# Causal mask of the short attention rows: added by VectorE in the score bank, where TensorE multiplied it in

## The chip, the cores and the metric

The kernel runs on one NeuronCore of a Trainium2 chip. A core has four compute engines that run their own instruction streams and meet at semaphores: TensorE (PE in the profile; PEld is its weight load), VectorE (DVE), ScalarE (ACT) and GpSimd (POOL). SyncE (SP) issues the DMAs. The metric is the device time of one execution in microseconds (us). The kernel before takes 1268.92 us, the median of three runs (1268.74 to 1269.92).

## The reference

One layer of a hybrid model on 512 tokens of width 1024, in float32: an input projection, a state-space branch, an attention branch with 16 heads in 4 key groups, a gated mix of the two, and an MLP. The attention branch adds three parts: over compressed keys, over selected blocks (there are 8 blocks and up to 16 are taken, so every causal block is), and over a window of 512 (the whole sequence). So the second and the third part are both plain causal attention, each with its own keys and values (ks, vs and kw, vw):

```python
def masked_softmax(s, m):
    p = jax.nn.softmax(jnp.where(m, s, NEG), axis=-1)
    return p * m
...
        s_s = jnp.einsum('bqgrd,bgqkd->bgrqk', qr, k_sel).astype(jnp.float32) * scale
        p_s = masked_softmax(s_s, m_s)
        o_s = jnp.einsum('bgrqk,bgqkd->bqgrd', p_s.astype(v_sel.dtype), v_sel)
...
        s_w = jnp.einsum('bqgrd,bkgd->bgrqk', qr, kwb).astype(jnp.float32) * scale
        p_w = masked_softmax(s_w, m_w)
        o_w = jnp.einsum('bgrqk,bkgd->bqgrd', p_w.astype(vwb.dtype), vwb)
```

Everything else of the layer is left as it is by the change.

## The kernel before, in words

**Tiling of the attention.** The 512 queries are cut into four blocks i = 0 to 3 of 128 rows. Block i sees (i + 1) * 128 keys, its width: 128, 256, 384 or 512. The work is cut into `PAIRS` = 64 pairs n = 0 to 63: pair n has a half rr = n // 32 of the heads, a query block that falls from 3 to 0 every 8 pairs, a key group g and a branch br (ks or kw). A pair holds two heads. Pairs of width 256 or 128 are called narrow: 16 to 31 and 48 to 63, 32 in all. A narrow pair has both heads side by side in one PSUM bank; a wide pair has a bank for each head.

**One pair, engine by engine.**
- `scores(n)` on TensorE: four products (two heads, the high and the low part of the keys) into the bank, then the causal table: for a narrow pair one product of the identity with the table `causal_bf`, 0 where a key is seen and -1e30 where it isn't, added to both diagonal blocks (line 2216). Its end raises `s_ready`. For a wide pair each head has its own (line 2213).
- `row_max(n)` on VectorE: waits for `s_ready`, takes the maximum of each row and negates it (`nmax`; line 1576 narrow, 1579 and 1582 wide).
- `exp(n, r2)` on ScalarE: the exponential with that bias, and its row sum (line 1004, with a short read of the sum behind it), one for each head.
- `over_sum(n)` on VectorE: one over the sum (`rsum`, line 1590).
- On GpSimd, line 854: the rows times `rsum` and the gate, one for each head (`prob`).
- `turn(n)` on TensorE: transposes (line 2248); `copy_turned` on ScalarE or VectorE (lines 1040, 1601, 1604): out of PSUM; `weigh(n)` on TensorE: times the values (2269), for odd n also the compressed part (2277). Then `high_out` on ScalarE (1011) and `low_out` on VectorE (1610) split the result of two pairs into a high and a low part.

**Order.** It is written out by hand in each engine's stream, and each engine keeps it strictly. `ahead` says how far scores run ahead: at an even narrow n the scores of n + 4 and n + 5 are issued (16 and 17 come at n = 13, 18 and 19 at 14). So two pairs make a round. In a round TensorE runs scores of the next two pairs, turns n and n + 1, weighs n - 2 and n - 1. VectorE runs `row_max` of both new pairs, `over_sum` of n + 2 and n + 3, a copy, `low_out`, and in three of four rounds some steps for the compressed part (`cmp_centre`, `cmp_probs`, `cmp_gates`; lines 1542 to 1568). ScalarE runs a copy, the four exponentials of the new pairs, and `high_out`. After pair 31 the wide pairs 32 to 47 follow, then the narrow pairs 48 to 63 in the same way, and then the state-space groups, the mix, w_o and the MLP.

**Steps on VectorE.** Where an instruction of VectorE needs what the one before it wrote, `step(...)` raises a semaphore of its own (`dve_steps`) and `step.wait()` waits for it.

Of the kernel before, what the change touches and what calls it, by code (L numbers as in the profile page):

```python
# [24 lines left out]
ALU = mybir.AluOpType  # L25
# [3 lines left out]
P = 128  # L29
# [43 lines left out]
K_ID, K_TRI, K_STRI, K_PERM, K_CB, K_CM, K_F = 0, 128, 256, 384, 512, 640, 768  # L73
# [62 lines left out]
def build(nc, a, out):  # L136

    ctx = ExitStack()
    with ctx:
        sem_names = {}  # L140

        def sem(name):
            return ctx.enter_context(nc.semaphore(name))
# [5 lines left out]
        def sb(name, shape, dt=F32, offset=None):  # L149
            size = 4 if dt in (F32, F32R, I32) else 2  # L150
            nbytes = (int(np.prod(shape[1:])) * size + 31) // 32 * 32
            where = at[0] if offset is None else offset
            if offset is None:
                at[0] += nbytes
            assert where + nbytes <= 229344, (name, where + nbytes)
            return nc.alloc_sbuf_tensor_at(name, list(shape), dt, offset=where)

        cst = sb("cst", [P, K_N])
# [7 lines left out]
        ident_bf = sb("ident_bf", [P, P], BF16)  # L166
        causal_bf = sb("causal_bf", [P, P], BF16)
# [73 lines left out]
        kk = [[sb(f"ks{part}", [P, KVG, S], F32R) for part in range(2)]]  # L241
# [16 lines left out]
        q_hl = sb("q_hl", [P, 16, S], F32R)  # L258
# [66 lines left out]
        bank = [ctx.enter_context(nc.psum_tensor(f"bank{i}", [P, 512], F32)) for i in range(8)]  # L325
# [67 lines left out]
        s_ready = sem("s_ready")  # L393
# [93 lines left out]
        def h_bank(k):  # L487

            return bank[(1, 0, 3, 4, 5, 6, 7, 2)[k]]
# [7 lines left out]
        def pair(n):  # L497

            return n // 32, NC - 1 - n // 8 % 4, n // 2 % 4, n % 2

        def width(n):
            return (pair(n)[1] + 1) * P

        def narrow(n):
            return width(n) <= 256
# [801 lines left out]
        def _(dve):  # L1307
            step = Steps(dve, dve_steps)
            V = nc.vector
# [38 lines left out]
            turned, less, part = (bank[2][:, i * P:(i + 1) * P] for i in (0, 2, 3))  # L1348
# [60 lines left out]
            for j in range(12):  # L1409
                u = U_KV + j  # L1410
# [11 lines left out]
                elif kind in (2, 4):  # L1422
                    b = kind // 4
# [147 lines left out]
            def row_max(n):  # L1571
                w, at_step = width(n), 2 * n % 16
                b, off = score_place[n][0]
                dve.wait_ge(s_ready, scored[n][0])
                if narrow(n):
                    V.tensor_reduce(nmax[:, at_step:at_step + 2], bank[b][:, 0:2 * w].rearrange("p (r k) -> p r k", r=2),
                                    AX.X, ALU.max, negate=True).then_inc(max_ready, 1)
                else:
                    V.tensor_reduce(nmax[:, at_step:at_step + 1], bank[b][:, 0:w], AX.X, ALU.max,  # L1579
                                    negate=True).then_inc(max_ready, 1)  # L1580
                    dve.wait_ge(s_ready, scored[n][1])
                    V.tensor_reduce(nmax[:, at_step + 1:at_step + 2], bank[score_place[n][1][0]][:, 0:w], AX.X, ALU.max,
                                    negate=True).then_inc(max_ready, 1)
# [29 lines left out]
            for u in range(6):  # L1613
# [7 lines left out]
                if u in (2, 4):  # L1621
                    cmp_read(0, u // 2 - 1)
            assert ahead[0] == [0, 1]
            row_max(0)
            cmp_centre(0)
            low_q(4)
            over_sum(0)
            cos_q(6)
            rope_q(5)
            row_max(1)  # L1630
            cmp_probs(0)
            cmp_gates(0)
# [400 lines left out]
        def _(pe):  # L2033
            T = nc.tensor
# [24 lines left out]
            for c in range(NC):  # L2059
                if c == 2:  # L2060
# [5 lines left out]
                             start=True, stop=True).then_inc(vec_turned, 1)  # L2066
                pe.wait_ge(xn_ready, c + 1)
                for k in range(KT - 1):
                    mm = T.transpose(h_bank(k)[:, c * P:(c + 1) * P], xn[:, c, k * P:(k + 1) * P], ident)
# [3 lines left out]
            for c in range(NC):  # L2073
                mm = T.transpose(h_bank(KT - 1)[:, c * P:(c + 1) * P], xn[:, c, D - P:D], ident)
# [37 lines left out]
            for j in range(12):  # L2112
                u = U_KV + j
# [5 lines left out]
                if j == 2:  # L2119
                    pe.wait_ge(unit_read[1], 1)  # L2120
                    for c in range(NC):
                        mm = T.transpose(bank[4][:, c * 48:(c + 1) * 48], ag[:, c * P:(c + 1) * P],
                                         ident[0:48, 0:48])
# [9 lines left out]
                if j == 10:  # L2133
                    pe.wait_ge(dta_spread, 3)
                    pe.wait_ge(kvc_ready, 2)
                    for c in range(NC):
                        mm = T.matmul(bank[2][:, c * P:(c + 1) * P], dta_wide[:, c, :], tri, start=True, stop=True)
# [3 lines left out]
                if j == 7:  # L2141
                    pe.wait_ge(hid_ready, 1)
                    for half in range(2):
                        mm = T.matmul(bank[2][:, 0:P], w2c[:, 0, half].rearrange("p e d -> p (e d)"),
                                      hid[:, 0, half].rearrange("p g k -> p (g k)"), start=(half == 0), stop=(half == 1))
                    mm.then_inc(kvc_summed, 1)
                if j == 11:

                    pe.wait_ge(hidr_ready, 1)
                    for g in range(KVG):  # L2150
                        for half in range(2):
                            mm = T.matmul(bank[3][:, g * HD:(g + 2) * HD], hidr[:, half, g].rearrange("p e k -> p (e k)"),
                                          w2c[:, 1, half].rearrange("p e d -> p (e d)"),
                                          start=(half == 0), stop=(half == 1))
# [41 lines left out]
            def scores(n):  # L2196
                rr, i, g, br = pair(n)
                pp, e = divmod(g, 2)
                w = width(n)
                for r2 in range(2):  # L2200
                    u = rr * 4 + 2 * pp + r2
                    b, off = score_place[n][r2]
                    if i == NC - 1 and br == 0:
                        pe.wait_ge(qlo_ready, 2 * u + 2)
                    if r2 == 0 or not narrow(n):
                        if score_free[n][r2]:
                            pe.wait_ge(exp_ready, score_free[n][r2])
                    for part in kk[br]:
                        T.matmul(bank[b][:, off:off + w], q_hl[:, 2 * u + e, i * P:(i + 1) * P], part[:, g, 0:w],  # L2209
                                 start=(part is kk[br][0] and off == 0), stop=(part is kk[br][1]),  # L2210
                                 skip_group_check=narrow(n))
                    if not narrow(n):
                        T.matmul(bank[b][:, i * P:(i + 1) * P], ident_bf[:], causal_bf[:],
                                 start=False, stop=True, skip_group_check=True).then_inc(s_ready, 1)
                if narrow(n):
                    T.matmul(bank[b][:, 0:2 * w].rearrange("p (r k) -> p r k", r=2)[:, :, i * P:(i + 1) * P], ident_bf[:],
                             causal_bf[:].unsqueeze(1).to_broadcast([P, 2, P]),
                             start=False, stop=True, skip_group_check=True).then_inc(s_ready, 1)

            def turn_to(k):  # L2220

# [284 lines left out]
            def turn_h2(k, c):  # L2506
                return T.transpose(h2_bank(k)[:, c * P:(c + 1) * P], xn2[:, c, k * P:(k + 1) * P], ident)


            for n, c in enumerate(WO_ORDER):  # L2510
                pe.wait_ge(xn2_first, n + 1)
                for k in range(KT // 2):
                    mm = turn_h2(k, c)
# [3 lines left out]
            for k in range(KT // 2, KT):  # L2517
                for c in range(NC):
                    mm = turn_h2(k, c)
# [72 lines left out]
```

## Time and profile before

| what | value |
|---|---|
| median of three runs | 1268.92 us |
| time of the profiled execution | 1269.1 us |
| its span | 1267.3 us |
| PE busy | 1247.1 us (98%) |
| DVE busy | 762.4 us (60%) |
| ACT busy | 583.3 us (46%) |
| POOL busy | 406.9 us (32%) |
| granted TensorE clock, mean | 0.998 |

The span runs from the first to the last instruction; the device time lies 1.8 us above it. Matmul ends are modelled in the profile, so a PE that reads 98% busy still has short gaps. The two narrow stretches lie at 205 to 241 us and at 282 to 317 us of the span.

### The profile page before, as it was taken

The page shows a single profiled execution, that of the slowest core. Times are in us where ns is not written, and L with a number is a line of the kernel's source. Part 1 is how long each engine was busy: PE and PEld are TensorE (multiplying, and loading weights), DVE is VectorE, ACT ScalarE, POOL GpSimd, SP SyncE. Part 2 cuts the span into 40 slices and gives each one's busy share as a digit, 9 for nine tenths or more (in the row PEclk, how much of TensorE's full clock was granted, in tenths as well). Part 3 has the DMA queues.
Part 4 walks back from the last instruction along what each step waited for, and adds up shares of the span by engine and source line. Part 5 has one row for each costly group of instructions (what it writes and reads, how often), then busy time and mean ns, then how long its engine had stood idle before and what let it go on. Part 6 is the DMA issues. An engine that isn't in the chain of part 4 may idle for free.

```text
span 1267.3 us, 19175 instructions
## 1 busy us (share of the span) xinstructions
PE 1247.1 (98%) x6732; PEld 1026.6 (81%) x6732; DVE 762.4 (60%) x1352; ACT 583.3 (46%) x1016; POOL 406.9 (32%) x271
## 2 busy tenths in 40 slices
PE   9999999999999999999999999999999999999997
PEld 7887877677888888888888888888878888888885
DVE  6845887775577877787874111111048849479487
ACT  6325476666544544454433222222366345254364
POOL 3433354545333333333333444444430110201200
PEclk9999999999999999999999999999999999999999
DMA  8523410000222222232222333334453061340601
GB/s 244 159 70 71 94 38 2 1 2 2 67 69 78 70 83 66 66 83 66 68 81 79 89 99 100 99 99 123 144 182 100 19 215 32 129 136 17 208 7 66
DMA packets 172312, 108.40 MB, mean 86 GB/s; under 512 B 25220, under 2 KB 163814, under 8 KB 172262
## 3 DMA queue, kind: packets, MB, share of 16 engines
q1 hardware_dynamic: 172022, 107.65, 29.2%
q8 instruction: 30, 0.49, 0.2%
q14 instruction: 20, 0.16, 0.0%
q10 hardware_dynamic: 240, 0.09, 0.0%
HBM read 104.84 MB, written 2.10 MB: 84 GB/s over the span
## 4 chain that ended last, share of the span: by engine, by line
PE 87%; DVE 4%; ACT 4%; issue 2%; POOL 1%; DMA 1%; SPq 0%; DVEq 0%; ACTq 0%; POOLq 0%
PE bank L2424 21%; PE bank L2046 17%; PE bank L2433 10%; PE bank L2050 9%; PE bank L2528 8%; PE bank L2533 4%; PE bank L2269 2%; PE bank L2443 2%; PE bank L2209 2%; PE bank L2248 2%; POOL prob L854 1%; PE bank L2106 1%; PE bank L2449 1%; PE bank L2404 1%; ACT prob L1004 1%
## 5 line engine op out<-in xcount | busy, mean ns | idle before, releaser
L834 POOL TENSOR_TENSOR wlo<-raw,whi 128x1024 fp32r<-128x1024 f32 x133 | 324.9, 2443 | 694.0 <-ACT whi L1082 388.5
L1082 ACT ACTIVATE whi<-raw 128x1024 fp32r<-128x1024 f32 x96 | 101.7, 1060 | 295.6 <-PE bank L2433 160.0
L2046 PE MATMUL bank<-h_hi,whi 128*128 128x512 f32 x488 | 194.5, 398 | 0.7 <-DVE h_lo L1323 0.7
L2046 PE MATMUL bank<-h_lo,whi 128*128 128x512 f32 x488 | 190.4, 390 | 0.0
L2424 PE MATMUL bank<-h_hi,whi 128*128 128x512 f32 x384 | 150.3, 391 | 1.3 <-DVE grp L1766 0.7
L2424 PE MATMUL bank<-h_lo,whi 128*128 128x512 f32 x384 | 149.5, 389 | 0.0
L2050 PE MATMUL bank<-h_hi,wlo 128*128 128x512 f32 x488 | 120.8, 390 | 0.0
L2046 PEld LDWEIGHTS bank<-h_hi,whi 128*128 128x128 f32 x488 | 91.8, 188 | 21.2 <-DVE h_lo L1323 2.5
L1854 DVE TENSOR_TENSOR mt<-bank,sig 128x512 f32<-128x512 f32 x16 | 11.1, 691 | 161.6 <-PE bank L2433 161.6
L1746 DVE SCALAR_TENSOR_TENSOR grp<-bank,vt,grp 128x511 f32<-128x511 f32 (+2 forms) x96 | 71.8, 748 | 58.9 <-ACT grp L1106 49.9
L2050 PEld LDWEIGHTS bank<-h_hi,wlo 128*128 128x128 f32 x488 | 91.6, 188 | 19.0
L2046 PEld LDWEIGHTS bank<-h_lo,whi 128*128 128x128 f32 x488 | 91.8, 188 | 17.6
L854 POOL TENSOR_SCALAR prob<-prob,rsum,gate 128x512 f32<-128x512 f32 (+3 forms) x128 | 79.5, 635 | 80.3 <-DVE rsum L1590 80.3
L2433 PE MATMUL bank<-h_hi,wlo 128*128 128x512 f32 x384 | 94.9, 389 | 0.0
L2424 PEld LDWEIGHTS bank<-h_hi,whi 128*128 128x128 f32 x384 | 72.1, 188 | 18.5 <-DVE h_lo L1894 2.7
L2433 PEld LDWEIGHTS bank<-h_hi,wlo 128*128 128x128 f32 x384 | 72.1, 188 | 15.0
L2424 PEld LDWEIGHTS bank<-h_lo,whi 128*128 128x128 f32 x384 | 72.1, 188 | 14.6
L1004 ACT ACTIVATE prob<-bank,nmax 128x512 f32<-128x512 f32 (+3 forms) x128 | 66.8, 535 | 37.1 <-DVE nmax L1579 33.8
L1234 ACT ACTIVATE whi<-raw 128x1024 fp32r<-128x1024 f32 x30 | 31.7, 1057 | 79.2 <-PE bank L2433 60.9
L1917 DVE TENSOR_TENSOR comb<-comb 128x256 f32<-128x256 f32 x64 | 30.2, 493 | 49.5 <-ACT comb L1272 49.0
L1967 DVE TENSOR_TENSOR x<-bank,x 128x512 f32<-128x512 f32 x64 | 41.1, 684 | 21.2 <-PE bank L2533 21.2
L2248 PE MATMUL bank<-cst,prob 128*128 128x128 f32 x320 | 48.6, 278 | 3.1 <-POOL prob L854 1.4
(318 smaller groups left out, 2502.2 us busy)
## 6 DMA issues: line engine op xcount, KB each, us to landing
raw<-in_w_in SPq DMA_DIRECT2D x75, 512.0 KB, 3.8
raw<-in_w_up SPq DMA_DIRECT2D x32, 512.0 KB, 4.1
draw<-in_w_down SPq DMA_DIRECT2D x16, 1024.0 KB, 6.5
raw<-in_w_ssm_branch SPq DMA_DIRECT2D x16, 512.0 KB, 3.6
raw<-in_w_in SPq DMA_DIRECT2D x20, 256.0 KB, 3.7
raw<-in_w_attn_branch SPq DMA_DIRECT2D x8, 512.0 KB, 3.6
raw<-in_w_o SPq DMA_DIRECT2D x8, 512.0 KB, 3.7
x_sb<-in_x SPq DMA_DIRECT2D x4, 512.0 KB, 5.3
```

The source lines that it names most:

```text
L834: nc.gpsimd.tensor_tensor(wlo[slot][:], raw[slot][:], whi[slot][:].bitcast(F32), ALU.subtract).then_inc(wlo_ready, units)
L854: nc.gpsimd.tensor_scalar(rows, rows, rsum[:, at_step % 16:at_step % 16 + 1], gate[:, i, column:column + 1], ALU.mult, ALU.mult).then_inc( ...
L1004: nc.scalar.activation(prob_rows(n, r2), bank[b][:, off:off + width(n)], ACT.Exp, bias=nmax[:, at_step % 16:at_step % 16 + 1], accum_out=e ...
L1082: nc.scalar.activation(whi[slot][:], raw[slot][:], ACT.Copy).then_inc(whi_ready, 1)
L1746: ins = V.scalar_tensor_tensor(grp[:, j, back:S], bank[j % 2][:, 0:S - back], vt[:, bass.ds(tile + (V_CW + (CONV - 1 - back) * 32), 1)], g ...
L2046: T.matmul(bank[slot][:], whi[slot][:, k * P:(k + 1) * P], part[:, k, :], start=(k == 0 and n == 0), stop=False)
L2050: mm = T.matmul(bank[slot][:], wlo[slot][:, k * P:(k + 1) * P], h_hi[:, k, :], start=False, stop=(k == KT - 1))
L2248: mm = T.transpose(to[:, off + t * P:off + (t + 1) * P], prob_rows(n, r2)[:, t * P:(t + 1) * P], ident)
L2424: T.matmul(to[:], whi[slot][:, k * P:(k + 1) * P], part[:, k0 + k, :], start=(start and k == 0 and n == 0), stop=False)
L2433: mm = T.matmul(to[:], wlo[slot][:, k * P:(k + 1) * P], hi[:, k0 + k, :], start=False, stop=(stop and k == KT - 1))
L2528: T.matmul(bank[at_bank + t][:], part[:, 2 * (n % 2) + kl, which, t * P:(t + 1) * P], half_slot(n, 0)[:, kl, :], start=(fresh and n % 2 == ...
L2533: return T.matmul(bank[at_bank + t][:], comb_hi[:, 2 * (n % 2) + kl, which, t * P:(t + 1) * P], half_slot(n, 1)[:, kl, :], start=False, st ...
```

## The change

For a narrow pair TensorE no longer multiplies the table in: its fourth score product raises `s_ready`. VectorE waits for that, adds the float32 table of `cst` (columns `K_CB` on) to the two diagonal blocks of the bank, in place, waits for its own step, and only then takes the maximum. Wide pairs are as before.

```diff
@@ row_max(n), on VectorE @@
                 dve.wait_ge(s_ready, scored[n][0])
                 if narrow(n):
+                    causal = bank[b][:, 0:2 * w].rearrange("p (r k) -> p r k", r=2)[:, :, w - P:w]
+                    step(V.tensor_tensor(causal, causal, cst[:, K_CB:K_CB + P].unsqueeze(1).to_broadcast([P, 2, P]), ALU.add))
+                    step.wait()
                     V.tensor_reduce(nmax[:, at_step:at_step + 2], bank[b][:, 0:2 * w].rearrange("p (r k) -> p r k", r=2),
                                     AX.X, ALU.max, negate=True).then_inc(max_ready, 1)
@@ scores(n), on TensorE @@
                     for part in kk[br]:
-                        T.matmul(bank[b][:, off:off + w], q_hl[:, 2 * u + e, i * P:(i + 1) * P], part[:, g, 0:w],
-                                 start=(part is kk[br][0] and off == 0), stop=(part is kk[br][1]),
-                                 skip_group_check=narrow(n))
+                        mm = T.matmul(bank[b][:, off:off + w], q_hl[:, 2 * u + e, i * P:(i + 1) * P], part[:, g, 0:w],
+                                      start=(part is kk[br][0] and off == 0), stop=(part is kk[br][1]),
+                                      skip_group_check=narrow(n))
...
                 if narrow(n):
-                    T.matmul(bank[b][:, 0:2 * w].rearrange("p (r k) -> p r k", r=2)[:, :, i * P:(i + 1) * P], ident_bf[:],
-                             causal_bf[:].unsqueeze(1).to_broadcast([P, 2, P]),
-                             start=False, stop=True, skip_group_check=True).then_inc(s_ready, 1)
+                    mm.then_inc(s_ready, 1)
```

On TensorE, in round n = 18 (scores of 22, here from its second head on, and of 23, then the transposes of 18), these are the rows before; `causal_bf,ident_bf` is the table product:

```order
L2209 MATMUL bank<-ks_102,q_hl 128x256
L2209 MATMUL bank<-ks_103,q_hl 128x256
L2216 MATMUL bank<-causal_bf,ident_bf 128x2x128
L2209 MATMUL bank<-kw_113,q_hl 128x256
L2209 MATMUL bank<-kw_114,q_hl 128x256
L2209 MATMUL bank<-kw_113,q_hl 128x256
L2209 MATMUL bank<-kw_114,q_hl 128x256
L2216 MATMUL bank<-causal_bf,ident_bf 128x2x128
L2248 MATMUL bank<-cst,prob_112 128x128 x4
```

and these the rows now (line 2212 was 2209, and 2249 was 2248):

```order
L2212 MATMUL bank<-ks_102,q_hl 128x256
L2212 MATMUL bank<-ks_103,q_hl 128x256
L2212 MATMUL bank<-kw_113,q_hl 128x256
L2212 MATMUL bank<-kw_114,q_hl 128x256
L2212 MATMUL bank<-kw_113,q_hl 128x256
L2212 MATMUL bank<-kw_114,q_hl 128x256
L2249 MATMUL bank<-cst,prob_112 128x128 x4
```

Two products less in the round; nothing else stands elsewhere on TensorE. On VectorE, from the `cmp_centre` steps ahead of round n = 18 to the `low_out` of its end, before:

```order
L1542 TENSOR_REDUCE cst_111<-cs 128x8
L1544 TENSOR_TENSOR cs<-cs,cst_111 128x2x128
L1576 TENSOR_REDUCE nmax<-bank 128x2 x2
L1590 RECIPROCAL rsum<-esum 128x2 x2
L1601 COPY pT_128<-bank 128x2x256
L1610 TENSOR_TENSOR o_lo<-bank,o_hi 128x128
```

and now (1577 is the add, 1579 was 1576, 1593 was 1590, 1604 was 1601, 1613 was 1610):

```order
L1542 TENSOR_REDUCE cst_111<-cs 128x8
L1544 TENSOR_TENSOR cs<-cs,cst_111 128x2x128
L1577 TENSOR_TENSOR bank<-bank,cst 128x2x128
L1579 TENSOR_REDUCE nmax<-bank 128x2
L1577 TENSOR_TENSOR bank<-bank,cst 128x2x128
L1579 TENSOR_REDUCE nmax<-bank 128x2
L1593 RECIPROCAL rsum<-esum 128x2 x2
L1604 COPY pT_128<-bank 128x2x256
L1613 TENSOR_TENSOR o_lo<-bank,o_hi 128x128
```

The two maxima that stood side by side now each have an add ahead of them, and the `rsum` of the earlier pairs, the copy and `low_out` stand behind all four.

## Rows read from the trace of the kernel before

**Rows 1.** Windows: engines' busy us (instructions), granted clock, DMA share, GB/s.
```profile
core 0: us, PE busy (x) PEld busy (x) DVE busy (x) ACT busy (x) POOL busy (x), PEclk, DMA share, GB/s
...
205.00:241.00 36.00, 34.62 (x321) 27.31 (x320) 24.92 (x75) 23.88 (x98) 19.33 (x37) 1.00 0.01 1
...
282.00:317.00 35.00, 33.86 (x321) 27.09 (x320) 21.37 (x66) 22.67 (x95) 19.27 (x38) 1.00 0.01 2
```

**Rows 2.** Waits, 205 to 241 us: waiter, awaited, total us, times, longest.
```profile
POOL prob L854 <- DVE rsum L1590: 14.8, 9, 2.7
DVE o_lo L1610 <- ACT o_hi L1011: 6.9, 8, 1.4
...
PEld bank L2248 <- POOL prob L854: 3.3, 9, 0.6
...
ACT prob L1004 <- DVE nmax L1576: 1.7, 3, 1.0
```

**Rows 3.** Chain that ended last, first narrow stretch: start us, us, what.
```profile
220.84 1.11 ACT prob L1004 x5
...
222.46 0.29 DVE o_lo L1610
...
223.65 0.62 DVE nmax L1576 x2
224.44 2.47 POOL prob L854 x4
```

**Rows 4.** Timeline of PE, round 18: start us, us, engine, line, what.
```profile
217.00 0.72 PE L2209 MATMUL bank<-ks,q_hl 128*128 128x256 f32 x4
...
217.60 0.72 PE L2209 MATMUL bank<-kw,q_hl 128*128 128x256 f32 x4
218.16 0.28 PE L2216 MATMUL bank<-causal_bf,ident_bf 128*128 128x256 bf16 x1
218.28 0.49 PE L2248 MATMUL bank<-cst,prob 128*128 128x128 f32 x3
```

**Rows 5.** Single lines: duration ns min/median/max, first and last start us, forms.
```profile
L1714 DVE TENSOR_TENSOR bank<-bank,eo x16: 566/566/567, 367.9 to 668.8; 128x384 f32<-128x384 f32 x16
...
L1371 DVE TENSOR_TENSOR bank<-bank,dtw x1: 299/299/299, 35.4 to 35.4; 128x128 f32<-128x128 f32 x1
```

**Rows 6.** Timeline of DVE: a step, and the instruction that waits for it.
```profile
367.94 0.57 DVE L1714 TENSOR_TENSOR bank<-bank,eo 128x384 f32<-128x384 f32 x1
368.54 0.69 DVE L1717 SCALAR_TENSOR_TENSOR yt<-bank,grp 128x512 f32<-128x512 f32 x1
```

**Rows 7.** Timeline of DVE, round 18.
```profile
218.30 0.29 DVE L1610 TENSOR_TENSOR o_lo<-bank,o_hi 128x128 fp32r<-128x128 f32 x1 [0.67 <-ACT o_hi L1011]
...
219.30 1.28 DVE L1576 TENSOR_REDUCE nmax<-bank 128x2 f32<-128x512 f32 x2
220.50 0.22 DVE L1590 RECIPROCAL rsum<-esum 128x2 f32<-128x2 f32 x2
```

**Rows 8.** Timeline of ACT: first exponentials and the high part behind them.
```profile
220.02 0.47 ACT L1004 ACTIVATE prob<-bank,nmax 128x256 f32<-128x256 f32 x1 [0.50 <-DVE nmax L1576]
...
223.97 0.37 ACT L1004 ACTIVATE prob<-bank,nmax 128x128 f32<-128x128 f32 x1 [1.00 <-DVE nmax L1576]
...
225.36 0.29 ACT L1011 ACTIVATE o_hi<-bank 128x128 fp32r<-128x128 f32 x1
```

**Rows 9.** Timeline of DVE: rsum and maxima in other rounds.
```profile
207.42 0.15 DVE L1590 RECIPROCAL rsum<-esum 128x2 f32<-128x2 f32 x1
...
223.56 0.70 DVE L1576 TENSOR_REDUCE nmax<-bank 128x2 f32<-128x256 f32 x2
...
234.05 0.22 DVE L1590 RECIPROCAL rsum<-esum 128x2 f32<-128x2 f32 x2
```

**Rows 10.** Timeline of POOL, last two groups of rows of the second stretch.
```profile
310.71 1.74 POOL L854 TENSOR_SCALAR prob<-prob,rsum,gate 128x128 f32<-128x128 f32 x4 [1.39 <-DVE rsum L1590]
312.78 1.75 POOL L854 TENSOR_SCALAR prob<-prob,rsum,gate 128x128 f32<-128x128 f32 x4 [0.32 <-DVE rsum L1590]
```

## The prediction

> **What bounds the kernel now.** The windows come first [rows 1]: the change touches two stretches, 36 and 35 us long. TensorE is 34.6 and 33.9 us busy in them, VectorE only 24.9 and 21.4, at the full 2.4 GHz clock (1.00). By shares the change takes work from the bound and gives it to an engine with 11.1 us of room (36.0 - 24.9). The waits contradict the shares [rows 2]: in the first stretch GpSimd waits 14.8 us for `rsum` of VectorE, VectorE 6.9 us for `o_hi` of ScalarE, and TensorE's weight loads 3.3 us for GpSimd. The chain shows what closes [rows 3]: exponentials at 220.84 (behind the maximum of 219.30 [rows 7]), `o_lo` at 222.46, the next maxima at 223.65, then `rsum` and GpSimd at 224.44, and TensorE behind it. That is a loop of VectorE and ScalarE through the hand-written orders: `low_out` waits for `high_out`, which stands behind the four exponentials on ScalarE; these wait for `row_max`, which stands behind the last `low_out`. So VectorE's 6.9 us is mostly the other half of a loop, not room.
>
> **What is removed.** 32 table products. In round 18 the scores of 22 start at 217.00, those of 23 at 217.60, the transposes at 218.28 [rows 4]. Four score products take 0.56 us (217.60 to the table product at 218.16), so 1.28 us for both pairs becomes 8 x 0.14 = 1.12: 0.16 us in a round. There are 16 rounds: 2.6 us, if TensorE set every one. That is the most that this part can give back. `s_ready` also comes 0.11 us earlier, which counts only where `row_max` waits for it.
>
> **What is added.** 32 adds of 128 x 256 in place in PSUM, each with a wait for its own result. The trace has the same form in two sizes: 566 ns for 384 and 299 ns for 128 elements [rows 5]; halfway is 433 ns. The instruction that waits starts 0.03 us behind the end: 367.94 + 0.57 = 368.51 against 368.54 [rows 6]. So a maximum starts 0.47 us later for its own add. Bounds for this: 0.30 (the 128-element form, no gap) and 0.60 (the 384-element form with its gap). I take 0.47, since both sizes stand on one line and 256 lies between them.
>
> Two maxima now run into each other: 1.28 us for both, the `rsum` 1.20 after the first start [rows 7]. An add without a wait would also hide 0.09 us in its neighbour (0.69 long, 0.60 apart). The Trainium skill ("VectorE: DVE Perf Modes", section The DRAIN you can't avoid) says that the next operation does not start before the pipeline is empty, with or without a semaphore. By that rule the wait is free and the add costs 0.43 - 0.09 = 0.34; the row of the step disagrees, since the dependent instruction starts behind the end and the independent maximum before it.
>
> **Which of it lies on the path.** In one round, `rsum` of the earlier pairs stands behind both adds: it is later than the round's start by 2 x 0.47 = 0.94 us. GpSimd and the transposes follow it. The next `low_out` is later by less, as ScalarE overlaps: it starts its first exponential 0.47 later, and then the second pair's maximum can be late too. At width 256 two exponentials take 0.9 us, the second maximum follows the first by 0.60 + 0.47 = 1.07, so 0.17 more; at width 128 the exponentials take 0.7 us (all four 225.36 - 223.97 = 1.39 us [rows 8]); the first maximum ends at 223.97, 0.41 behind its start, and both take 0.70 [rows 9], so the second follows by 0.29 + 0.47 = 0.76, 0.1 more. A round that VectorE leads, which shows as ScalarE idle before its first exponential (three times [rows 2], 0.50 at 220.02 and 1.00 at 223.97 [rows 8]), thus adds 0.6. Where `low_out` waited for something else, that wait takes the delay up first.
>
> Round by round in the first stretch, delay at `low_out` and then at `rsum`:
> - Scores of 16 and 17: the adds follow pair 15's maxima directly. `rsum` at 207.42 [rows 9] comes 0.94 - 0.11 = 0.83 later. The `low_out` behind it waited for ScalarE and takes up about half, so some 0.4 stays.
> - 18 and 19: 0.39, then 1.33. GpSimd is late by that and TensorE's transposes of 15 behind it.
> - 20 and 21: TensorE's scores come 1.33 - 0.16 = 1.17 later; `rsum` 1.17 + 0.94 = 2.11.
> - 22 and 23: `low_out` 1.17 (218.30 [rows 7]), `rsum` at 220.50 later by 2.11. TensorE had waited for GpSimd here already, so it takes the whole.
> - 24 and 25: VectorE leads: 1.17 + 0.64 = 1.81; `rsum` (behind the maxima of 223.56 [rows 9]) 2.75.
> - 26 and 27: it leads again: 1.81 + 0.58 = 2.39; `rsum` 3.3.
> - 28 and 29: `high_out` waits for TensorE, late by 2.75; I take 3.45 for `rsum`, not 3.7, since scores of this round come while VectorE runs its maxima, and part of the wait for them goes.
> - 30 and 31: `low_out` 2.6, `rsum` at 234.05 [rows 9] 3.5.
>
> GpSimd was idle before that last step and TensorE waited for it, so the transposes of 28, the weighing and the scores of 32 are 3.5 us late. The wide pairs behind are bound by TensorE and give nothing back. TensorE's 0.16 a round is in these numbers and mostly lost: it waits for GpSimd instead.
>
> The second stretch has the same order as the first up to the scores of pair 61, and I take the same delays. At its end GpSimd starts its last group 0.32 us after the one before ended [rows 10]. The first of these is 3.4 late (310.71 becomes 314.09); it takes 1.78 and the last then follows without a gap at 315.87 in place of 312.78: 3.1 late, and so are the last transposes and the first product behind the attention.
>
> **Sum.** 3.5 + 3.1 = 6.6 us. The profiled execution, 1269.1 us with a span of 1267.3, would be 1275.7 with a span of 1273.9. The median of the runs lies 0.2 below: 1275.5. With 0.30 for an add instead of 0.47 the sum scales to 4.2 (1273.1), with 0.60 to 8.4 (1277.3); if the joints between rounds take up 1.5 us more or less, that is 1271.6 to 1278.8. Elsewhere in the program nothing moves.
>
> **The rivals.**
> - *TensorE sets the end after all.* VectorE's idle 11.1 us [rows 1] holds 16 x 0.47 = 7.5 us of adds. If that idle time is real room, only the 0.16 us a round is left: 1268.9 - 2.6 = 1266.3, faster. For it speaks TensorE's 34.6 of 36 us; against it GpSimd's 14.8 us of waiting for `rsum` [rows 2] and the loop in the chain. It decides if ScalarE does not wait for the maxima: it did, in the rows quoted.
> - *The joints take up most.* ScalarE waits for the narrow maxima three times only [rows 2]; if the other rounds absorb their 0.94 (the `low_out` waits are up to 1.4 us [rows 2]), 0.6 x 3 a stretch less TensorE's 1.3 is left: 0.5 a stretch, 1270. Against it: `rsum` is delayed in each round directly, and TensorE's loads wait for GpSimd nine times [rows 2].
> - *Nothing is taken up.* Each add delays everything behind it: 32 x 0.47 = 15.0, 1283.9. Against it: ScalarE's four exponentials overlap the second add.
> - *The wait is free*, as by the pipeline rule: 6.6 x 0.34 / 0.47 = 4.8, 1273.7. The row of the step speaks against it.
> - *TensorE's clock falls.* The gaps in which it waits for GpSimd grow from 0.6 [rows 2] to some 1.3 us. The granted clock is 1.00 in both stretches now; no row of this kernel shows the 1.2 GHz level behind such gaps. If a third of one stretch ran at it, its 12 us of products would take up to twice as long: about 1287.
>
> **How the numbers follow.** A measurement of this kernel can tell about 0.2% (2.5 us) from no change: the bounds are 1266.4 and 1271.5. Chances: the forecast 0.66 (own range 1271.6 to 1279); TensorE sets the end 0.06; the joints take up most 0.08; nothing is taken up 0.11; the wait is free 0.05; the clock 0.04. Low end 1270.5, which leaves out the first rival and half of the second; high end 1281, which leaves out the clock and most of the third. Faster 0.06; same 0.08 and 0.01 of the forecast's lower tail; slower 0.85.
>
> **What would show it.** Right: 32 adds of 0.43 us, each maximum 0.03 us behind its add; the second maximum no longer overlapping the first; `rsum` of the eight rounds later by 0.8, 1.3, 2.1, 2.1, 2.75, 3.3, 3.45, 3.5 us against a common start; TensorE's idle time before the transposes larger, released by GpSimd; the first wide scores 3.5 us later, the first product after the attention 6.6 later, and the same lag at the end. Wrong: a narrow stretch no longer than 36.5 us, or one 7 us longer; an add under 0.3 or above 0.6 us; a granted clock under 1.00 in a stretch; a lag that shrinks in the wide pairs or after the attention.

## The result, and the profile after

| | before | after |
|---|---|---|
| median of the runs (6 each) | 1268.93 us | 1276.91 us (1276.06 to 1277.84) |
| ratio to before | | 1.006 [1.0051, 1.007] |
| profiled execution, its span | 1269.1, 1267.3 us | 1276.6, 1274.8 us |
| granted clock, mean of the span | 0.998 | 0.995 |

The changed kernel is slower by 8.0 us, 0.6% and well outside the scatter of either kernel; 6.6 was forecast.

The adds, by their line in the changed kernel (duration ns min/median/max, first and last start us):

```profile
L1577 DVE TENSOR_TENSOR bank<-bank,cst x32: 406/423/433, 205.9 to 317.6; 128x256 f32<-128x256 f32 x32
```

VectorE of the changed kernel at the head of the first stretch and in round 18 (start us, us, engine, line, what), to be laid beside [rows 7, 9]:

```profile
205.89 0.43 DVE L1577 TENSOR_TENSOR bank<-bank,cst 128x256 f32<-128x256 f32 x1
206.36 0.69 DVE L1579 TENSOR_REDUCE nmax<-bank 128x2 f32<-128x512 f32 x1
206.97 0.42 DVE L1577 TENSOR_TENSOR bank<-bank,cst 128x256 f32<-128x256 f32 x1
...
208.03 0.16 DVE L1593 RECIPROCAL rsum<-esum 128x2 f32<-128x2 f32 x1
...
219.00 0.29 DVE L1613 TENSOR_TENSOR o_lo<-bank,o_hi 128x128 fp32r<-128x128 f32 x1 [0.67 <-ACT o_hi L1011]
...
220.00 0.43 DVE L1577 TENSOR_TENSOR bank<-bank,cst 128x256 f32<-128x256 f32 x1
220.46 0.69 DVE L1579 TENSOR_REDUCE nmax<-bank 128x2 f32<-128x512 f32 x1
...
222.13 0.22 DVE L1593 RECIPROCAL rsum<-esum 128x2 f32<-128x2 f32 x2
```

An add is 0.43 us long and its maximum starts 0.03 to 0.04 us behind the end of the add. The two maxima no longer follow each other directly. TensorE in the same round, beside [rows 4]:

```profile
217.70 0.72 PE L2212 MATMUL bank<-ks,q_hl 128*128 128x256 f32 x4
218.26 0.64 PE L2212 MATMUL bank<-kw,q_hl 128*128 128x256 f32 x4
218.74 0.98 PE L2249 MATMUL bank<-cst,prob 128*128 128x128 f32 x6
```

From the scores of 22 to the transposes it now takes 1.04 us (217.70 to 218.74) and took 1.28. The waits, 205 to 244 us (waiter, awaited, total us, times, longest), beside [rows 2]:

```profile
POOL prob L854 <- DVE rsum L1593: 17.4, 9, 2.9
PEld bank L2249 <- POOL prob L854: 8.0, 18, 1.4
...
DVE o_lo L1613 <- ACT o_hi L1011: 5.4, 7, 1.6
ACT prob L1004 <- DVE nmax L1579: 4.2, 5, 1.2
```

TensorE's weight loads waited 3.3 us for GpSimd and now wait 8.0; ScalarE waits 4.2 us for the narrow maxima instead of 1.7. This window is 3 us longer than that of before, as the stretch itself is.

**Where the time went.** Marks in TensorE's timeline of the kernel before: the last wide scores (of the branch kw, the attention over a window) ahead of the first stretch, the transposes of 28, the first wide scores behind the stretch, the last wide scores ahead of the second stretch, and the first product behind the attention.

```profile
204.38 0.59 PE L2209 MATMUL bank<-kw,q_hl 128*128 128x384 f32 x2
...
234.81 1.62 PE L2248 MATMUL bank<-cst,prob 128*128 128x128 f32 x4 [0.35 <-POOL prob L854]
...
237.20 0.71 PE L2209 MATMUL bank<-ks,q_hl 128*128 128x512 f32 x2
...
281.45 0.59 PE L2209 MATMUL bank<-kw,q_hl 128*128 128x384 f32 x2
...
316.67 0.48 PE L2046 MATMUL bank<-h_hi,whi 128*128 128x512 f32 x1
```

The same marks in the changed kernel:

```profile
204.18 0.60 PE L2212 MATMUL bank<-kw,q_hl 128*128 128x384 f32 x2
...
237.74 1.77 PE L2249 MATMUL bank<-cst,prob 128*128 128x128 f32 x4 [1.19 <-POOL prob L854]
...
240.94 1.20 PE L2212 MATMUL bank<-ks,q_hl 128*128 128x512 f32 x2
...
286.43 0.59 PE L2212 MATMUL bank<-kw,q_hl 128*128 128x384 f32 x2
...
324.30 0.47 PE L2049 MATMUL bank<-h_hi,whi 128*128 128x512 f32 x1
```

Against a common first mark (the changed kernel was 0.20 early there) the delay is 237.74 - 234.81 + 0.20 = 3.13 us at the transposes of 28, 286.43 - 281.45 + 0.20 = 5.18 at the second stretch, and 324.30 - 316.67 + 0.20 = 7.83 behind the attention. So the first stretch gives 3.13 and the second 2.65. The 2.05 between them come in the first wide pairs. There two score products of 512 columns take 1.20 us instead of 0.71, and the windows of the changed kernel say why (busy us of the engines PE, PEld, DVE, ACT and POOL, then the granted clock):

```profile
236.00:238.00 2.00, 0.81 (x7) 0.44 (x3) 1.48 (x6) 1.71 (x9) 0.77 (x2) 0.97 0.03 8
238.00:244.00 6.00, 5.95 (x23) 3.66 (x23) 3.56 (x12) 1.94 (x7) 2.72 (x7) 0.50 0.00 0
244.00:246.00 2.00, 2.00 (x16) 1.09 (x14) 1.28 (x3) 1.37 (x4) 0.00 (x0) 0.82 0.00 0
```

The granted clock falls from 1.00 to 0.50 (1.2 GHz) at about 237.9, right behind TensorE's idle 1.19 us before 237.74, and is back at 1.00 some 6.8 us later, at about 244.7.

### The profile page after: what moved, and what is told of

Same layout as the page of the kernel before. It is cut to its first block, busy times and chain, and to the rows that moved or that the text cites. A ratio compares the mean times of both kernels' runs of the same rounds, so it can differ in the third digit from the quotient of the medians.

```text
span 1274.8 us, 19143 instructions
## 1 busy us (share of the span) xinstructions
PE 1249.6 (98%) x6700; PEld 1025.2 (80%) x6700; DVE 775.3 (61%) x1384; ACT 585.6 (46%) x1016; POOL 406.7 (32%) x271
## 4 chain that ended last, share of the span: by engine, by line
PE 87%; DVE 5%; ACT 3%; issue 2%; POOL 1%; DMA 1%; SPq 0%; DVEq 0%; ACTq 0%; POOLq 0%
PE bank L2425 20%; PE bank L2049 17%; PE bank L2434 10%; PE bank L2053 8%; PE bank L2529 8%; PE bank L2534 4%; PE bank L2270 2%; PE bank L2212 2%; PE bank L2444 2%; PE bank L2249 2%; POOL prob L854 1%; PE bank L2109 1%; PE bank L2450 1%; PE bank L2405 1%; PE bank L2316 1%
## 5 line engine op out<-in xcount | busy, mean ns | idle before, releaser
L2249 PE MATMUL bank<-cst,prob 128*128 128x128 f32 x320 | 52.1, 283 | 7.8 <-POOL prob L854 5.6
```

The costliest lines, as they stand in the source:

```text
L2249: mm = T.transpose(to[:, off + t * P:off + (t + 1) * P], prob_rows(n, r2)[:, t * P:(t + 1) * P], ident)
```

## The experiments

Two theories stood at the start. One: the adds stand ahead of `rsum` on VectorE, GpSimd starts later by them, TensorE waits for it, and its own saved products don't count. The other: what costs is TensorE's clock, or an add whose cost doesn't depend on what stands behind it. The letters A, B and C in a forecast below are its own. Each kernel has 5 to 11 runs. The experiments ran in three groups of four, each on another chip, each beside the kernel before: this had 1268.95 us in the first group (the changed kernel again, the gap filled, neither product nor add, the second stretch only), 1269.49 in the second (both, `rsum` ahead, `o_lo` last on the changed kernel) and 1269.29 in the third (the rest). The changed kernel itself ran in the first group alone. Where a later kernel is set against its 1276.62, the two come from different chips, which leaves about 0.5 us open; the ratios are to the kernel before on the same chip.

**The changed kernel again.** No edit.

> The changed kernel once more, beside the three that are compared with it. Expected 1276.9 us again (1276.0 to 1277.9). In its first profile the lag behind the kernel before is 3.1 us at the transposes of pair 28 (237.74 against 234.81, starts of the attention 0.2 apart), 5.2 in the wide pairs and 7.6 at the first product behind the attention; the 2 us between the first two lie where the granted clock was 0.50. Theory A (the clock falls each time behind the gap before the transposes of pair 28): the same 2 us and the same place again. Rival B (a chance event of that one execution): full clock in this profile and a span shorter by 2 us.

Measured: 1276.62 us (1275.94 to 1277.76), 1.006 [1.0046, 1.0074]. Its windows:

```profile
205.00:245.00 40.00, 35.82 (x310) 26.64 (x308) 31.96 (x94) 25.65 (x100) 19.76 (x38) 1.00 0.00 1
...
304.00:310.00 6.00, 5.71 (x37) 4.50 (x38) 4.51 (x14) 3.15 (x14) 3.65 (x7) 0.72 0.01 3
...
318.00:324.00 6.00, 5.37 (x30) 3.62 (x32) 1.67 (x7) 1.75 (x9) 3.28 (x8) 0.72 0.01 3
```

The first stretch kept the full clock; two falls of some 3.4 us each came in the second. So falls recur from execution to execution and their place does not, and neither A nor B of this forecast holds. The marks of this execution price them:

```profile
204.90 0.59 PE L2212 MATMUL bank<-kw,q_hl 128*128 128x384 f32 x2
...
238.45 1.62 PE L2249 MATMUL bank<-cst,prob 128*128 128x128 f32 x4 [1.20 <-POOL prob L854]
...
285.11 0.59 PE L2212 MATMUL bank<-kw,q_hl 128*128 128x384 f32 x2
...
324.68 0.47 PE L2049 MATMUL bank<-h_hi,whi 128*128 128x512 f32 x1
```

Against the common first mark (0.52 late) the delay is 3.12 us at the transposes of 28 and still 3.14 at the second stretch: with the clock at 1.00 the wide pairs add nothing, so the 2.05 us of the first execution go with its fall. Behind the attention it is 7.49, so the second stretch gives 4.35 with two falls where it gave 2.65 with none, 1.7 us for both.

**The gap before the transposes of 28 filled**, with products into the bank that the transposes overwrite.

```
+                if n == 28:
+                    to = turn_to(turn_no[n][0])
+                    for _ in range(5):
+                        T.matmul(to[:], q_hl[:, 0, 0:P], q_hl[:, 0, :], start=True, stop=True)
```

> The changed kernel, with five products of 128x512 on TensorE ahead of the transposes of pair 28, written to the bank that these transposes overwrite and read by nobody; they fill the gap of 1.19 us that TensorE has there (5 x 0.22 us = 1.1). Theory A (the gap lets the clock fall and that costs 2 us): granted clock 1.00 from 236 to 245 us, lag of the wide pairs 3.2 instead of 5.2 us, time 1274.9 us. Rival B (the clock falls by chance or for another reason, or the 2 us are the lag of the loop in another place): 1276.9 us as without the fillers, or 0.1 to 0.3 more.

Measured: 1275.02 us (1274.87 to 1276.31), 1.0049 [1.0035, 1.0063], 1.6 below the changed kernel on the same chip. Both windows of its profile have the full clock:

```profile
205.00:245.00 40.00, 37.02 (x315) 27.46 (x313) 32.13 (x93) 25.70 (x101) 19.75 (x38) 1.00 0.00 1
286.00:325.00 39.00, 35.55 (x308) 27.06 (x307) 28.99 (x86) 23.43 (x93) 18.64 (x36) 1.00 0.01 2
```

The attention ends at 322.47 there, 5.74 us late against the common first mark (204.44): near 3.1 + 2.65, the delay of the two stretches alone. A (1274.9) held. About 1.6 us of the 8.0 go with the filled gap; the marks put them in the clock. The runs of the two kernels overlap at their ends (up to 1276.31 here, from 1275.94 there). That one filled gap takes away falls elsewhere too is not shown: they vary.

**Neither product nor add**: the mask of the narrow pairs is left out.

```
-                    T.matmul(bank[b][:, 0:2 * w]..., ident_bf[:], causal_bf[:]..., start=False, stop=True, ...).then_inc(s_ready, 1)
+                    mm.then_inc(s_ready, 1)
```

> The products of the table are gone and no add takes their place: the causal mask of the 32 narrow pairs is left out of the computation. It shows what TensorE's part of the change is worth alone. Loop theory (VectorE and ScalarE lead the round where ScalarE waits for the maxima, TensorE leads the others): less than the 2.6 us of 16 rounds x 0.16, I expect 1.5 us, 1267.4 us. Rival (TensorE sets the end of every round): 2.6 us, 1266.3 us. Rival (TensorE sets none): 1268.9 us.

Measured: 1267.69 us (1267.47 to 1268.55), 0.999 [0.9981, 0.9999]: -1.26 us. That is all that 32 table products are worth on the path, of 8 x 0.24 + 8 x 0.20 = 3.5 us that they occupy on TensorE (1.28 us less 1.04 in a round of width 256, 1.12 less 0.92 in one of width 128). It lies between the two rivals and near the 1.5 of the forecast.

**Both product and add** (the table is added twice).

```
+                    causal = bank[b][:, 0:2 * w].rearrange("p (r k) -> p r k", r=2)[:, :, w - P:w]
+                    step(V.tensor_tensor(causal, causal, cst[:, K_CB:K_CB + P]..., ALU.add))
+                    step.wait()
```

> The kernel before with VectorE's add and its wait put in, and TensorE's product with the table kept (the table is added twice, so the output is another). It prices VectorE's part alone. Taking TensorE's table product out with no add in its place gave -1.26 us. Theory A (VectorE's add delays rsum, GpSimd starts that much later, and TensorE, waiting for GpSimd anyway, has no time of its own on that path): the product's absence is worth little once the adds are there, so this kernel stands 0 to 1.3 us above the changed one, 1276.6 to 1277.9. Rival B (TensorE's time counts one for one beside the adds): 32 products of about 0.24 us beyond the changed kernel's, 1276.6 + 7.7 = 1284. Rival C (the add alone costs nothing, and what costs is the score bank that is handed over sooner): about 1269.

Measured: 1277.35 us (1276.76 to 1278.14), 1.0063 [1.0049, 1.0077]. With the adds there, TensorE's table products cost 0.7 us against the changed kernel's 1276.62, and 0.2 if each is set against the kernel before on its own chip (7.86 against 7.67): not clear of noise. The forecast priced B twice too high, since 0.24 us is the saving for the two products of a round: at the 3.5 us above, B would stand at 1280.1. It is out at that price too, and so is C: the add on VectorE alone makes the loss.

**Adds in the second stretch only** (pairs 48 to 63; the first keeps its products). VectorE's add has the same condition.

```
-                if narrow(n):
+                if narrow(n) and n >= 48:
```

> The table is added by VectorE for pairs 48 to 63 only; pairs 16 to 31 keep their product on TensorE. The second stretch cost 2.65 us in the changed kernel (lag 4.98 before it, 7.63 behind it). Theory A (each stretch pays for itself, the first one 3.1 in the loop and 2.0 in the clock): 1268.9 + 2.65 = 1271.6 us, clock 1.00 in both. Rival (half of the change costs half, 4 us): 1272.9 us.

Measured: 1272.51 us (1272.29 to 1273.45), 1.0027 [1.0017, 1.0038]: +3.6, between the two forecasts, 0.9 above A and 0.4 below the rival. Its profile has +2.60 from the start of the second stretch to the end of the attention, at full clock, as the changed kernel had 2.65. So the second stretch pays this by itself and doesn't need the first. The profile loses 1.0 us more between 325 and 600 us, where the edit changes nothing and the other profiles lose nothing; where that comes from stays open.

**`rsum` ahead of the adds and maxima**, on the changed kernel and on the kernel before.

```
             for n in range(PAIRS):
+                if ahead[n + 1] and narrow(ahead[n + 1][-1]):
+                    for m in due:          # the pairs whose sums this round owes
+                        over_sum(m)
                 for m in ahead[n + 1]:
                     row_max(m)
```

> The changed kernel with VectorE's reciprocals of the row sums that are due in a round (rsum) put ahead of the round's adds and maxima instead of behind them. In the changed kernel's trace of round 18 the exponentials of these sums had ended at 218.80, rsum started at 222.13, and the adds and maxima that stand ahead of it had started at 220.00: it could start 2.1 us sooner. Theory A (the cost is that rsum, and so GpSimd, stands behind the adds): nearly all of the 7.7 us goes away, and with GpSimd early some of TensorE's waits for it too: 1268, within 1265.5 to 1270.5. Rival B (VectorE's added time itself, or the exponentials behind the later maxima, holds the rounds): each maximum comes 0.14 us later still, about 1277 to 1279. Rival C (both count): halfway, 1272 to 1274.

> The kernel before with the same move of rsum ahead of the round's maxima, and TensorE's table products kept. Theory A: GpSimd's start comes 1.1 to 1.3 us sooner in each round, and TensorE's waits for it in the two stretches (8.1 us of first waits together by the earlier trace) shrink: 1266, within 1263.5 to 1268.4. Rival B (GpSimd's start doesn't hold the rounds of the kernel before, since there TensorE or the exponentials do): the same or up to 1 us more, 1268.9 to 1270.

Measured: the changed kernel 1272.56 us (1272.25 to 1273.89), 1.0028 [1.0017, 1.004], so -4.1 against 1276.62, and 3.1 above the kernel before on its own chip; the kernel before 1266.65 us (1266.28 to 1267.69), 0.9976 [0.9967, 0.9985], so -2.8 (A, 1266, held). VectorE in round 18 of the changed kernel with `rsum` ahead:

```profile
218.21 0.29 DVE L1613 TENSOR_TENSOR o_lo<-bank,o_hi 128x128 fp32r<-128x128 f32 x1 [0.66 <-ACT o_hi L1011]
...
219.20 0.22 DVE L1593 RECIPROCAL rsum<-esum 128x2 f32<-128x2 f32 x2
219.34 0.41 DVE L1577 TENSOR_TENSOR bank<-bank,cst 128x256 f32<-128x256 f32 x1
219.78 0.69 DVE L1579 TENSOR_REDUCE nmax<-bank 128x2 f32<-128x512 f32 x1
```

and one of its waits, 205 to 244 us:

```profile
ACT prob L1004 <- DVE nmax L1579: 6.0, 5, 1.6
```

`rsum` comes 1.0 us behind the start of `o_lo`, not 3.1. But ScalarE's wait for the maxima grew from 4.2 to 6.0 us: that speaks for the other arc of the loop, maxima to exponentials. Theory A said 1268 and fell; the halfway case (C, 1272 to 1274) held. Not all of the gain is the loop's: this profile has the full clock in both stretches, and against the common first mark (204.18) it is 1.67 us late at the second stretch (282.92) and 3.39 behind the attention (319.86). So the stretches cost 1.67 and 1.72 where they cost 3.13 and 2.65: `rsum` ahead takes 2.4 of 5.8 us from the loop, and the 2 us at the lower clock are absent from this execution. The later maxima are the candidate for the 3.4 that stay.

**`o_lo` last in its round**, on the changed kernel and on the kernel before.

```
-                if n % 2 == 1 and n >= 3:
-                    low_out((n - 3) // 2)
                 ...
                 if n % 8 == 5 and n < 61:
                     cmp_gates(n // 8 + 1)
+                if n % 2 == 1 and n >= 3:
+                    low_out((n - 3) // 2)
```

> The changed kernel with VectorE's subtraction o_lo put last in its round, behind the steps of the compressed branch (centre, probs, gates) instead of ahead of them. In the trace of the changed kernel VectorE waits there 0.67 us (219.00) and 0.84 us (223.78) for ScalarE's o_hi, 5.4 us in the first stretch, with 0.8 us of that branch's steps queued behind it that wait for nothing. Theory A (each round's rsum is late by what stands ahead of it on VectorE, waits included): the steps fill the wait, rsum comes 0.4 to 0.8 us sooner in three of four odd rounds, and the time falls by 2 to 4 us, 1272.5 to 1274.6. Rival B (VectorE's wait is slack that comes back elsewhere): the same within 0.5 us, 1276.6.

> The kernel before with o_lo last in its round, rsum where it was. Theory A (rsum's lateness holds this kernel's rounds as well, only less): VectorE's wait for o_hi is filled by the compressed branch's steps, rsum comes 0.4 to 0.7 us sooner, and with rsum ahead of the maxima worth 2.5 us this is worth 1 to 2.5: 1266.5 to 1268. Rival B (in this kernel the maxima and the rsum are early enough): no change, 1269.

Measured: the changed kernel 1272.44 us (1271.59 to 1273.96), 1.0024 [1.0015, 1.0033], so -4.2 against 1276.62, and 3.0 above the kernel before on its own chip; the kernel before 1266.20 us (1265.18 to 1266.92), 0.9975 [0.9966, 0.9984], so -3.1. Both times A's mechanism held and the gain came out just above its range. The move applies to the wide pairs too, so the gain is not the narrow stretches' alone. Round 18 of the changed kernel with this edit:

```profile
218.04 0.41 DVE L1542 TENSOR_REDUCE cst<-cs 128x8 f32<-128x256 f32 x1
218.48 0.45 DVE L1544 TENSOR_TENSOR cs<-cs,cst 128x256 f32<-128x256 f32 x1
218.85 0.28 DVE L1613 TENSOR_TENSOR o_lo<-bank,o_hi 128x128 fp32r<-128x128 f32 x1
219.05 0.42 DVE L1577 TENSOR_TENSOR bank<-bank,cst 128x256 f32<-128x256 f32 x1
```

and its wait:

```profile
DVE o_lo L1613 <- ACT o_hi L1011: 2.0, 2, 1.1
```

The steps of the compressed branch fill the idle 0.67 us ahead of `o_lo`, and the next add starts directly behind it; the wait for `o_hi` goes from 5.4 to 2.0 us. Part of VectorE's idle time was thus a wait with ready work queued behind it.

**Each add twice.**

```
                     step(V.tensor_tensor(causal, causal, cst[:, K_CB:K_CB + P]..., ALU.add))
                     step.wait()
+                    step(V.tensor_tensor(causal, causal, cst[:, K_CB:K_CB + P]..., ALU.add))
+                    step.wait()
```

> The changed kernel with VectorE's add and its wait done twice for each of the 32 pairs (the table is added twice, so the output is another). It asks how much cover VectorE's first add used up. An add and the gap behind it measure 0.46 us (205.89 to 206.36), two in a row 0.43 + 0.46. Theory A (the first add used up what cover there was: GpSimd waits for rsum in every round and starts the moment it comes): the second add passes nearly whole, 32 x 0.45 = 14 us, 1276.6 + 14 = 1291, within 1288 to 1293. Rival B (each add costs what the first did, about half of it covered): 1276.6 + 7.7 = 1284. Rival C (the first's cost was a wait that is paid once a round, whatever its length): under 1280.

Measured: 1294.36 us (1293.17 to 1297.02), 1.0194 [1.018, 1.0208]: +17.7 us over the changed kernel, 0.55 for each of 32 adds that take 0.46 with their gap. The number is above the range of A, and its profile has long falls of the clock, so the sum alone doesn't price a second add. A part at full clock does: from the first exponential of pair 20 to that of pair 24 it takes 231.54 - 220.33 = 11.21 us, and the changed kernel 225.78 - 216.86 = 8.92. Four second adds make 2.29 us, 0.57 each. So no cover is left for a second add, and B and C are out. The windows (the first holds most of that part; how much the falls cost in all is not measured apart):

```profile
218.00:231.00 13.00, 10.81 (x96) 8.20 (x98) 10.59 (x27) 6.68 (x23) 4.35 (x8) 1.00 0.01 2
...
234.00:246.00 12.00, 11.59 (x70) 9.54 (x70) 8.58 (x26) 5.10 (x22) 4.81 (x11) 0.57 0.00 0
```

**Both moves on VectorE**: `rsum` ahead and `o_lo` last.

> The changed kernel with both moves on VectorE: rsum ahead of the adds and maxima, and o_lo last in its round. Each alone gave -4.1 us (1272.56 and 1272.44). Theory A (both shorten the same path, from VectorE's wait for o_hi through rsum to GpSimd; but after the first the exponentials wait for the maxima, 6.0 us of ScalarE's idle time in the first stretch, and that wait the second move takes away): together -6 to -8, 1268.6 to 1270.6, about the kernel before. Rival B (TensorE then has no wait left and its saved table products show): below the kernel before with rsum moved, under 1266.6. Rival C (they remove the same wait): no more than either alone, 1272.

> The kernel before with both moves. With rsum moved alone it took 1266.65, TensorE was busy 39.4 of 40 us of the first stretch and waited for GpSimd 2.0 us in first waits of 0.3 at most. Theory A (TensorE is the bound there): nothing more to be had, 1266.6 within 0.6 us. Rival B (the second stretch, where TensorE was busy 38.2 of 39, and its exponentials' waits for maxima still hold it): 1265.5.

Measured: the changed kernel 1268.81 us (1267.66 to 1271.76), 0.9995 [0.9986, 1.0004]; the kernel before 1264.92 us (1263.87 to 1265.24), 0.996 [0.9947, 0.9974]. On the changed kernel the moves add up for the most part (-4.1, -4.2, together -7.8; against the kernel before on each chip they leave 3.1, 3.0 and -0.5 of 7.7) and take back the whole loss, without making it clearly faster than before: A held. On the kernel before they give -4.4 us, the fastest version here. There the forecast A of no gain over the first move was wrong and its rival B (1265.5) the nearer one: TensorE was not yet the bound. The first window of that kernel, and the same of the changed kernel:

```profile
205.00:245.00 40.00, 39.56 (x374) 31.91 (x374) 29.67 (x86) 28.50 (x112) 22.58 (x42) 1.00 0.01 1
```

```profile
205.00:245.00 40.00, 36.06 (x290) 26.60 (x288) 30.45 (x90) 24.83 (x97) 19.07 (x37) 0.91 0.00 1
```

TensorE busy 39.56 of 40 us is close to its bound; 36.06 is not. With both moves in both, the change still costs 1268.81 - 1264.92 = 3.9 us. The profile with the moves and the adds, the slowest of its 11 runs, has a fall of its own:

```profile
286.00:314.00 28.00, 24.82 (x243) 20.15 (x241) 22.38 (x71) 19.48 (x81) 16.64 (x34) 1.00 0.01 2
314.00:322.00 8.00, 7.90 (x33) 5.79 (x33) 3.06 (x7) 0.73 (x3) 0.23 (x1) 0.57 0.00 0
```

But 3.55 us of difference stand ahead of that fall: the first exponential of pair 60 comes 307.17 - 205.08 = 102.09 us behind the first mark there, and 303.42 - 204.88 = 98.54 in the kernel before with both moves. So most of the 3.9 us is the loop's and not the clock's. That it is the later maxima is argued; no run moves them alone.

## Why the prediction was right, point by point

- **What bounds the stretches** (a loop of VectorE and ScalarE, VectorE's idle time no room). Right. The table products off TensorE give 1.26 us, the adds on VectorE alone take 7.9 (1277.35 against 1269.49), and reordering VectorE's own instructions takes the loss back.
- **An add, 0.43 us and 0.03 behind it.** Measured 0.423 and 0.03 to 0.04. The dependent maximum starts behind the end of its add (205.89 + 0.43 = 206.32 against 206.36), while the add behind a maximum that it doesn't depend on starts 0.08 us before that one's end (206.36 + 0.69 = 207.05 against 206.97). The rule weighed against the row, of the Trainium skill ("VectorE: DVE Perf Modes", section The DRAIN you can't avoid), by which the semaphore costs nothing extra, thus did not hold here. The same section of the Trainium skill also says that an operation that is not held starts earlier, which this add bears out.
- **TensorE gives back at most 0.16 us a round.** Mis-sized: 0.24 at width 256 (1.28 to 1.04) and 0.20 at width 128 (1.12 to 0.92). The 0.16 took 0.56 us for each group of four products; the second group, with the transposes directly behind it, takes 0.48 (218.26 to 218.74), the first 0.56. "Mostly lost" was right: 3.5 us freed, 1.26 of it worth anything without the adds and 0.2 to 0.7 with them.
- **`rsum`, round by round.** Forecast 0.83, 1.33, 2.11, 2.11, 2.75, 3.3, 3.45, 3.5. Measured, with the 0.20 of the common mark: 0.81, 1.15, 1.96, 1.83, 2.47, 3.22, 3.10, 3.12 (207.42 to 208.03 the first, 234.05 to 236.97 the last). The order of the delays, their two steps where VectorE leads and their levelling at the end came as worked out; from the second on each is 0.1 to 0.4 less, in line with the 0.04 to 0.08 a round that TensorE gives back beyond the forecast.
- **The first stretch 3.5, the second 3.1.** Measured 3.13 and 2.65, with GpSimd's last groups run together as forecast: the 0.32 us of [rows 10] are gone. (The forecast's 1.78 us for a group is 1.75 in the row, which moves nothing.)

```profile
318.67 3.47 POOL L854 TENSOR_SCALAR prob<-prob,rsum,gate 128x128 f32<-128x128 f32 x8 [1.29 <-DVE rsum L1593]
```

- **The wide pairs give nothing back.** Right at the full clock: 3.12 and 3.14 us at their two ends in the second execution. In the first they added 2.05 us at the lower clock.
- **The clock, as a rival at 0.04 and 1287.** Here the forecast had its gap. It priced a fall over a third of a stretch; what came is a fall of some 6.8 us, behind nearly the gap that the prediction named (1.19 us where it said 1.3), worth 1.6 to 2. A granted clock under 1.00 in a stretch was among its signs of being wrong, and it came. The mechanism belonged inside the sum, as a small term, and not in a rival with a large one.
- **The sum.** 5.8 us by the two stretches where 6.6 stood, and about 2 by the clock where nothing stood, make 7.8. The two errors are of opposite sign: that 6.6 lies as near to 8.0 as it does is in part luck.
- **The rivals.** TensorE sets the end: out, by the run without product and add, -1.26, and the run with both, +7.9. The joints take up most: out by the round-by-round delays. Nothing is taken up: out for one add (8 of 15 us), true for a second one. The wait is free: out by the rows above.
- **Two arcs of the loop.** The prediction has the adds delay `rsum` by 0.94 us in a round, and through the first exponentials the next round by some 0.6. With `rsum` moved ahead of the adds 3.1 us of loss remain (3.4 in the profile, at full clock), so the second arc exists; that it runs through the maxima to the exponentials fits ScalarE's waits (4.2 to 6.0 us), and no run isolates it.

## What to carry to other kernels

Moving work from the busiest engine to one with idle time pays only if that idle time isn't the far half of a loop. Look at what the idle engine waits for, and at what is queued behind the new instruction there. Here the largest gain lay in the order of an engine's own queue: a result that another engine waits for goes ahead of long operations that don't feed it, and an instruction that must wait goes behind those that need not (4.4 us of 1269, with no work saved). When a change opens gaps before TensorE, put a small term for its clock into the sum.

## What the runs showed of the hardware that was not expected

- TensorE's granted clock went from 1.00 to 0.50 right behind an idle gap of 1.19 us (the changed kernel, before 237.74). In the second execution the same gap, 1.20 us before 238.45, left it at 1.00; there it fell at 306.1, 2.1 us behind the end of a gap of 0.46 us, and at 319.7, 1.4 us behind the end of one of 0.41 us.
- Falls are not the adds' alone. The profiles of four kernels have one of some 3.4 us between 923 and 935 us, far behind the attention, three of them without any add (the mask left out, `rsum` ahead on the kernel before, both moves on the kernel before) and one with (`o_lo` last on the changed kernel). TensorE idles there 0.88 and 0.90 us a little before. The kernel before idles 0.87 and 0.90 us in the same place and kept the full clock. The kernel before with both moves, and then the kernel before:

```profile
923.00:927.00 4.00, 3.83 (x20) 3.83 (x21) 1.97 (x4) 3.20 (x7) 0.00 (x0) 0.57 0.00 0
```

```profile
924.00:930.00 6.00, 4.23 (x33) 3.37 (x32) 3.31 (x9) 5.52 (x13) 0.00 (x0) 1.00 0.28 83
```

- With both moves on the changed kernel a fall that began in the attention (at about 314.3) reached into the dense products behind it, of which each took 0.63 us at first and 0.40 later:

```profile
318.55 0.63 PE L2056 MATMUL bank<-h_lo,whi 128*128 128x512 f32 x1
...
321.34 0.40 PE L2056 MATMUL bank<-h_hi,whi 128*128 128x512 f32 x1
```

- Single runs spread by 4.1 us with both moves on the changed kernel and by 3.9 us with each add twice, whose profiles have falls in the attention, and by 1.4 us in the kernel before with both moves, whose profile has falls too, but elsewhere. Not all scatter is the clock's: executions already differ ahead of the first stretch, where the same scores start at 204.66 us in the changed kernel and at 205.67 in that with both product and add.
